# Second layer norm in a feed-forward kernel: its scaling moves to ScalarE, its shift to GpSimd, its tiles to other steps

## The reference, cut to what matters

```python
h = layer_norm(DEEPNORM_ALPHA * h + mix, ln1_g, ln1_b)
ff = (jax.nn.silu(h @ w_ff_gate) * (h @ w_ff_up)) @ w_ff_down
return layer_norm(DEEPNORM_ALPHA * h + ff, ln2_g, ln2_b)

def layer_norm(x, g, b, eps=1e-5):
    mu = jnp.mean(x, -1, keepdims=True); xc = x - mu
    var = jnp.mean(xc * xc, -1, keepdims=True)
    return xc * lax.rsqrt(var + eps) * g + b
```

## Time and profile before

| | us |
|---|---|
| median of 3 runs | 3842.73 (3835.66 to 3848.98) |
| the profiled run: device time | 3841.75 |
| its span, first to last instruction | 3839.5 |
| down stage on PE, from first to last matmul | about 3364 to 3812 |
| after the last matmul | about 3812 to 3839.5 |

### The profile page before, as it was taken

How to read it: one execution, slowest core, us unless ns; L and a number is a source line. 1 busy time by engine, 2 the same in 40 slices (tenths; PEclk the granted TensorE clock), 3 DMA queues, 4 the chain that set the end, 5 groups by cost and what they waited for, 6 DMA issues and landing times. The chain is left out here.

```text
span 3839.5 us, 52628 instructions
## 1 busy us (share of the span) xinstructions
PE 3512.5 (91%) x17866; PEld 2925.5 (76%) x17866; DVE 2162.0 (56%) x2906; ACT 1901.6 (50%) x3569; POOL 1742.2 (45%) x2034
## 2 busy tenths in 40 slices
PE   5998788898979999999997998889999999999896
PEld 4876566676767888989996877678887888888685
DVE  4206666787522365567442665565456545466857
ACT  3213577787624698888554332243334333344342
POOL 5313566665411132222002665556665665454544
PEclk9989899899986999999998999999999999999998
DMA  7324322422221111100004455654445444465562
GB/s 241 150 66 111 83 74 70 157 83 82 88 91 36 40 40 42 35 26 15 19 15 141 144 173 198 212 179 169 153 163 174 164 139 144 156 247 187 207 228 97
DMA packets 327963, 464.23 MB, mean 121 GB/s; under 512 B 22809, under 2 KB 216553, under 8 KB 323849
## 3 DMA queue, kind: packets, MB, share of 16 engines
q1 hardware_dynamic: 301296, 417.88, 32.9%
q10 hardware_dynamic: 26400, 43.00, 3.2%
HBM read 307.02 MB, written 153.78 MB: 120 GB/s over the span
## 5 line engine op out<-in xcount | busy, mean ns | idle before, releaser
L2454 POOL TENSOR_TENSOR ff_rounded_ring<-ff_raw,ff_rounded_ring 128x512 fp32r<-128x512 f32 x264 | 380.2, 1452 | 297.6 <-ACT ff_rounded_ring L2588 295.0
L105 PE MATMUL ff_bank<-ff_rounded_pair,ff_rounded_ring 128*128 128x512 f32 x1232 | 482.8, 392 | 18.6 <-DVE ff_resid L2748 7.6
L106 PE MATMUL ff_bank<-ff_rounded_pair,ff_rounded_ring 128*128 128x512 f32 x1232 | 481.6, 391 | 0.0
L107 PE MATMUL ff_bank<-ff_rounded_pair,ff_rounded_ring 128*128 128x512 f32 x1232 | 481.5, 391 | 0.0
L1643 PE MATMUL at_ctx<-at_p_t,at_c_nat 128*128 128x128 f32 (+1 forms) x2432 | 351.9, 286 | 7.9 <-ACT at_ctx_t L1754 7.0
L1643 PEld LDWEIGHTS at_ctx<-at_p_t,at_c_nat 128*128 128x128 f32 (+1 forms) x2432 | 306.5, 194 | 37.7 <-ACT at_ctx_t L1754 13.0
L1748 ACT ACTIVATE at_p_t<-at_turn 128x512 f32<-128x512 f32 (+4 forms) x416 | 213.1, 544 | 206.5 <-PE at_turn L1621 172.7
L2459 POOL TENSOR_TENSOR ff_rounded_ring<-ff_raw,ff_rounded_ring 128x512 fp32r<-128x512 f32 x154 | 215.3, 1404 | 186.5 <-ACT ff_rounded_ring L2638 186.4
L105 PEld LDWEIGHTS ff_bank<-ff_rounded_pair,ff_rounded_ring 128*128 128x128 f32 x1232 | 232.8, 189 | 69.7 <-POOL ff_rounded_ring L2454 16.3
L2816 DVE TENSOR_TENSOR ff_rounded_a_ring<-ff_f_q,ff_rounded_a_ring 128x512 fp32r<-128x512 f32 x154 | 199.3, 1301 | 135.6 <-ACT ff_rounded_a_ring L2630 134.4
L107 PEld LDWEIGHTS ff_bank<-ff_rounded_pair,ff_rounded_ring 128*128 128x128 f32 x1232 | 232.7, 189 | 49.0
(11 more groups left out here) (360 smaller groups left out, 9095.8 us busy)
## 6 DMA issues: line engine op xcount, KB each, us to landing
f_kept<-ff_resid SPq DMA_DIRECT2D x154, 256.0 KB, 2.5
ff_f_q<-f_kept SPq DMA_DIRECT2D x14, 2816.0 KB, 10.2
pj_raw<-in_w_in SPq DMA_DIRECT2D x50, 512.0 KB, 4.4
proj<-se_row SPq DMA_DIRECT2D x96, 256.0 KB, 2.2
ff_raw<-in_w_ff_gate SPq DMA_DIRECT2D x22, 1024.0 KB, 10.7
ff_raw<-in_w_ff_up SPq DMA_DIRECT2D x22, 1024.0 KB, 6.3
ff_raw<-down_comb SPq DMA_DIRECT2D x88, 256.0 KB, 2.7
ff_raw<-in_w_ff_down SPq DMA_DIRECT2D x66, 256.0 KB, 3.2
```

Source lines behind the costliest of these rows:

```text
L105: pe.matmul(out, lhs_lo, rhs_hi, start=start, stop=False, skip_group_check=goes_on)
L106: pe.matmul(out, lhs_hi, rhs_hi, start=False, stop=False, skip_group_check=goes_on)
L107: return pe.matmul(out, lhs_hi, rhs_lo, start=False, stop=stop, skip_group_check=goes_on)
L2454: pool.tensor_tensor(ring[:, step % RING, 1, :].rearrange("p (k c) -> p k c", c=P), f_operand(it, q, m), f32(ring[:, step % RING, 0, :]).r ...
```

## The change

1. **The norm is split over three engines.** `center` on DVE keeps the statistics and the subtraction with the gain. `scale` on ACT multiplies by the root, `add_shift` on POOL adds the shift; both are 128x1024 in place. The tiles stand at other steps, three and four apart: 67, 70, 74, 78 for `resid[0]` of pass 0, 82, 86, 90, 94 for its `resid[1]`, and 144, 147, 149, 151 for `resid[0]` of pass 1. For a tile at D, DVE centres it in its loop at D, POOL takes the root at D+1, ACT scales at D+2, POOL shifts at D+3, ACT stores at D+5.
2. **The last four tiles.** The statistics of their second half, complete earlier, are taken inside the loop (`half_statistics`, steps 145, 148, 150, 152). After the loop, DVE gathers and centres tile by tile. Tiles 0 and 2 are scaled by ACT and shifted by POOL, tiles 1 and 3 by DVE as before (`scale_and_shift`).
3. **Residuals by tile.** `resid[0]` for pass 1 is asked for in four DMAs of 512 KB, at SP's d = 75, 78, 82, 86, each after the store of that tile. `resid[1]` is still one DMA, at SP's d = 103 instead of 99.
4. **Down operands.** `load_product` goes from SP to ACT (`load_late_product`), still at k = 8 of the issuer's loop. ACT's loop stands three steps later in time than SP's.

```diff
+        after = NI * (NQ - 1)
+        NORMS = {after + k: (0, 0, a) for a, k in enumerate((1, 4, 8, 12))} | {after + k: (0, 1, a) for a, k in enumerate((16, 20, 24, 28))}
+        NORMS |= {after + NI * NQ + k: (1, 0, a) for a, k in enumerate((1, 4, 6, 8))}
+        HALF_STATS = {after + NI * NQ + k: a for a, k in enumerate((2, 5, 7, 9))}
...
+                def load_resid_tile(a):
+                    sp.wait_ge(out_stored[a], 16 + START)
+                    sp.dma_start(resid[0][:, a, :], h1_nat[2][:, a * D:a * D + D]).then_inc(resid_loaded[0], 16)
...
-                    if k == 8 and n + 2 < NPASS * NQ:
-                        load_product(n + 2)
-                    if p == 1 and q == 0 and k == 4:
-                        sp.wait_ge(out_stored[0], 16 * TPG + START)
-                        load_resid(1, 0)
-                    if p == 1 and q == 2 and k == 0:
-                        sp.wait_ge(out_stored[1], 16 * TPG + START)
+                    if NORMS.get(d - 8, (1, 0, 0))[:2] == (0, 0):
+                        load_resid_tile(NORMS[d - 8][2])
+                    if p == 1 and q == 2 and k == 4:
+                        sp.wait_ge(out_stored[TPG], 16 * TPG + START)
                         load_resid(1, 1)
...
+                def add_shift(p, h, a):
+                    pool.wait_ge(scaled2, norm_index(p, h, a) + 1 + START)
+                    pool.tensor_tensor(resid[h][:, a, :], resid[h][:, a, :], ln[1][:, :], ALU.add).then_inc(h2_ready, 1)
...
-                for a in range(TPG):
-                    inverse_root(NG + 2 * NPASS - 1, a)
+                add_shift(NPASS - 1, 0, 3)
+                last = NG + 2 * NPASS - 1
+                inverse_root(last, 0)
+                inverse_root(last, 1)
+                add_shift(NPASS - 1, 1, 0)
+                inverse_root(last, 2)
+                add_shift(NPASS - 1, 1, 2)
+                inverse_root(last, 3)
...
+                def scale(p, h, a):
+                    act.wait_ge(centered2, norm_index(p, h, a) + 1 + START)
+                    act.wait_ge(rstd_ready, TPG * (NG + 2 * p + h) + a + 1 + START)
+                    act.activation(resid[h][:, a, :], resid[h][:, a, :], ACT.Copy, scale=rstd[:, a:a + 1]).then_inc(scaled2, 1)
...
+                    if k == 8 and n + 2 < NPASS * NQ:
+                        load_late_product(n + 2)
+                    if d - 2 in NORMS:
+                        scale(*NORMS[d - 2])
+                    if d - 5 in NORMS:
+                        store_out(*NORMS[d - 5])
...
                 for a in range(TPG):
                     gather(NPASS - 1, NQ - 1, a)
-                dve.drain()
-                for a in range(TPG):
-                    normalize(NG + 2 * NPASS - 1, resid[1], a, h2_ready)
+                    dve.drain()
+                    center(NPASS - 1, 1, a)
+                    if a == 2:
+                        scale_and_shift(1)
+                scale_and_shift(3)
```

83 lines of the change are left out of this document (62 added, 21 removed).

## The result

The changed kernel takes 3822.12 us (median of 8 runs, 3812.79 to 3829.7) against 3842.1 us for the kernel before on the same chip (8 runs). The ratio is 0.9942, 95% interval 0.9931 to 0.9954: 20 us less, where 29.4 were forecast. Its profiled run took 3820.59 us, with a span of 3818.8. Both intervals exclude 1, so the gain is clear of the noise, though it is only 0.6% of the whole. Direction and range were right; the forecast gain was 9 us too large in the first measurement and 6 in the second.

A forecast was written before the change was run, and what follows sets the result against it. PE bounds the down stage, with DVE taking time from it at the norms. Gains of 22.9 + 4.2 + 4.3 less 2 make 29.4 us, giving 3813.3 us against the runs' median; range 3804 to 3830.

The forecast's parts named there:

- The middle and the late loss: Down stage: 22.9 us lost between loops 68 and 145, 4.2 us from loop 145 to the end; both expected gone.
- The tail's chain: After the last matmul: root 3 behind tile 2's shift, then `scale_and_shift(3)`; 23.0 us, gain 4.3, between 2 and 6.
- the residue of 2 us: Stalls left in the down stage from POOL and DVE slowing each other: 2 us, with ends of 0 and 6.
- The losses taken as gone: Down stage: PE's losses around the norms and in the last product, 27.1 us together, less a residue.
- the signs that I had named for being wrong: PE waiting for L2889 in steps 82 to 97, ACT waiting for weights near step 83, or the last stage not shorter.
- those for being right: Among others: no DVE-ended PE idle in steps 67 to 100, clock 1.00 there, no PE pause at pass 0's end.
- The sum per four steps: DVE and POOL work in four loop steps: 10.9 to 11.5 us, up to 0.7 more than available; cover 5.4.
- At step 77 no tile is being centred ... the 6.3 us go as well.: End of pass 0: gathers run as PE's sums come in, so PE's 6.3 us wait for a gather disappears.
- I expect small transfers to be as late next to it as before: DMA: moving the product request to ACT's queue leaves small transfers beside it as late as before; no gain.
- Rival 1: Loop norms: a root holds DVE off as the shift did; gain only 14.4, time 3828; chance 0.12.
- Rival 2: Weights late after SP's longer wait at tile 1: PE pauses some 5 us, gain 22.4, time 3820; chance 0.08.
- Rival 3: Steps 67 to 97: coupling of three engines puts DVE or POOL behind per tile; slower, 3860; chance 0.04.

The follow-up runs named there:

- e3: Changed kernel with the loop's tiles back at the old steps, two apart, the norm still split over three engines; 3820.17 us, ratio 0.9948.
- e4: Changed kernel with the new steps, but DVE alone normalising each whole tile of the loop; 3831.07 us, ratio 0.9972.
- e2: Changed kernel without POOL's shift for the twelve tiles in the loop, whose output lacks that addition; 3809.16 us, ratio 0.9914.
- e9: Changed kernel with four one-element-per-partition powers on POOL in place of each loop tile's shift; 3818.47 us, ratio 0.9938.
- e1: Changed kernel with the product request back on SP, at k = 8 of its own loop; 3821.54 us, ratio 0.9944.
- e10: Changed kernel with each loop tile's shift in two halves on POOL and the pass 0 end gathers ahead of that loop's `low_a`; 3820.62 us, ratio 0.9944.
- e5: Changed kernel with each loop tile's shift in two halves on POOL at successive steps; 3818.48 us, ratio 0.9933.
- e6: Changed kernel with the four gathers at the end of pass 0 put ahead of that loop's `low_a` on DVE; 3818.15 us, ratio 0.9929.
- e11: Changed kernel unaltered, measured again in later rounds; 3818.44 us, ratio 0.9937 to the kernel before.
- e12: Changed kernel with half of each loop tile's shift (columns 512 to 1023) moved from POOL to DVE; 3826.58 us, ratio 0.9953.

## Why the prediction was right, and where its size failed

**Right: what bounded the kernel, and that the split removes it.** The middle and the late loss were waits for DVE at the norms. The late loss is gone whole: 26.18 of 26.2 us busy. e3 and e4 show that it is the split. The tail's chain ended with the predicted pieces in the predicted order, at 23.4 us against 23.0; its gain was 3.9 us against 4.3, within the bounds given. Here some luck was in it: my working had root 1 end 7.5 us after PE; it ended 10.0 us after it, behind the centring of tile 0 (3.27 us, which I had counted as 1.3), and the later pieces made up most of that.

**Failed: the residue of 2 us.** The losses taken as gone were 27.1 us, which from 448.0 leaves 420.9. The down stage took 428.3 and 430.6 us in two profiles: the residue is 7.4 to 9.7 us. My ends for it were 0 and 6, so the total came into the range only because the range was wide. Of the signs that I had named for being wrong, one came: PE still waits for L2889 at step 94 (1.5 us). Of those for being right, two failed: PE pauses at the end of pass 0, and the clock of the stretch is 0.98. Three steps were wrong.

*The sum per four steps compared an average with a cover.* It found DVE and POOL together 0 to 0.7 us short in four steps, and set 5.6 us in eight tiles against a cover of 5.4. But it is the lag within a tile that PE meets at a place without cover. With a shift beside it a `low_a` took 2.88 us, and tile 2 was begun 2.7 us later than in an undisturbed step (T(74) + 5.5 instead of 2.8), partly since ACT stood waiting for a root with the features of the next step behind it, which I had put at nothing. e2 shows the price: without the shift the same stage takes 422.5 us. The Trainium skill, *SBUF — State Buffer*, section "SBUF: two separate sides", gives the rule that a DVE instruction with two SBUF inputs and a GpSimd one that reads SBUF exclude each other for the whole instruction; the row at 3572.42 agrees with it. e9 suggests that this is not the whole price, since PE waited 2.5 us for POOL's low weights there, without any shift in the loop.

*"At step 77 no tile is being centred ... the 6.3 us go as well."* Only 2.3 of them went in the first profile. What I overlooked is that DVE's queue is in order: the gathers stand behind two `low_a` and the centring of loop 74, which even undisturbed end 1.0 us too late (e2 measured 1.2). The nearest tile in step numbers was not the nearest in time.

*"I expect small transfers to be as late next to it as before."* They came later. The weights asked for at 3571.97, behind the product's 2816 KB and a residual tile, landed 13.2 us later (11.0 at most in the kernel before), and ACT waited 4.8 us for them at step 77; at step 89 it waited 6.2 us, and the pause at step 94 stands behind that wait. In all, ACT's waits for weights grew from 35 to 55 us. At the one place that I had worked out, near step 83, ACT did not wait.

**The rivals.** Rival 1, the shared port, gave 3828 for a root that holds DVE off as a shift does. This did not come: a root ran beside a centring that kept its 1.27 us. It is the root that was held off,

```profile
3566.99 1.27 DVE L2829 SCALAR_TENSOR_TENSOR ff_resid<-ff_resid,ff_mv,ff_ln 128x1024 f32<-128x1024 f32 x1
3567.16 1.52 POOL L2446 TENSOR_TENSOR ff_rstd<-ff_ve,ff_half 128x1 f32<-128x1 f32 x1 [0.81 <-DVE ff_ve L2828]
```

for it ended 0.4 us after the centring, and took 1.52 us where it takes 0.55 alone (last section). My sum had taken the 1.52 us as POOL's own work. A milder form of the rival, by the shift alone, is part of the missing gain. The time came to lie between the forecast and this rival. Rival 2, late weights, named 3820 and so the right time, mostly for a wrong reason: the waits for weights did grow, from 35 to 55 us, but the largest pause has none ahead of it. At one place they do take part: ahead of the 1.5 us pause at step 94, ACT had waited 6.15 us for weights, and POOL's shift and two `low_b` came on top. Rival 3 did not come in its size, though its coupling over ACT did, as said. That the move of the product request costs nothing and gains nothing was right in the time (e1: 3821.54 us); the late weights only changed their step.

**The distance.** I gave the steps three and four apart a share in the gain, as free time per tile (4.1 to 5.4 us against 3.0). e3 and e4 show it to be small: 0 to 3 us on top of the split, 4.6 alone.

## What to carry to other kernels

When one engine has no time left at some steps, count not only how much an instruction takes from it, but where its lag meets a consumer without buffer; there the queue of the engine, item by item, gives the delay, and an average over several steps hides it. Work that reads two large tiles from SBUF is not moved off DVE for free by giving it to GpSimd; measure the version without the work (e2) first, since it bounds all rearrangements. And when a pause is removed at one place, look at the whole stage's time before believing the gain, and at who ended each new pause, through to the end of the chain: here three versions took 1.3 to 3.4 us from one pause and gained none, and the releaser that PE's row names for the largest new one (`low_a`) had itself been waiting for a transfer. The same holds for an experiment that should rule a rival out: e1 moved the late weights to the very place that it was to clear of them.

## What the runs showed of the hardware

A power of one element per partition on POOL takes 0.55 us when it starts while DVE runs no instruction with two large SBUF inputs (`low_a`, centring, or scaling with shift). Started behind one, it ended 0.41 us after that instruction. This held for every such start with more than 0.15 us of the DVE instruction left, in the down stages and tails of all fourteen profiles: so the 1.52 us of a root are 1.11 us of waiting for the centring, and the 1.00 us of the first of e9's powers are 0.59 us of waiting for a `low_a`. In e9, the first with DVE idle, the second two with a `low_a` begun 0.14 us behind a power:

```profile
3611.31 0.55 POOL L2447 TENSOR_TENSOR ff_rstd<-ff_ve,ff_half 128x1 f32<-128x1 f32 x1
...
3618.64 3.09 POOL L2478 TENSOR_TENSOR ff_junk<-ff_half 128x1 f32<-128x1 f32 x4
3619.93 0.68 DVE L2896 TENSOR_TENSOR ff_rounded_a_ring<-ff_f_q,ff_rounded_a_ring 128x512 fp32r<-128x512 f32 x1
```

The `low_a` was not held off by the power: it took 0.68 us, as it does alone. So the wait goes one way for so small an operand, and both ways for large ones. The two `low_b` behind e9's powers took 3.85 us (2.99 behind a shift) since the first of them began beside a centring, not because powers stood ahead.

A gather, which reads one tile of SBUF and one accumulator, is not held off by POOL, nor POOL by it. In e9:

```profile
3573.56 3.03 DVE L2924 SCALAR_TENSOR_TENSOR ff_resid<-ff_resid,ff_bank 128x512 f32<-128x512 f32 x4
3573.84 1.28 POOL L2472 TENSOR_TENSOR ff_rounded_ring<-ff_raw,ff_rounded_ring 128x512 fp32r<-128x512 f32 x1
```

The granted clock did not fall behind every pause. At the end of pass 0 the matmuls went on at full distance after pauses of 0.6, 1.2 and 1.8 us (e10, e2, e9). After 2.3 and 2.7 us (e5, e6) the distances of 0.43 us cost 1.7 and 1.3 us more, after 4.0, 3.7 and 4.3 us (changed, e11, e12) 1.7, 2.9 and 2.5. But the length of the pause alone does not decide it: a pause of 2.7 us at step 91 of e10 was followed by matmuls at full distance, and one of 1.9 us at step 8 of e6 by 1.7 us of loss at the lower clock. The pauses of the table therefore do not sum to the stage's loss: 418.9 us (154 x 2.72) and 6.7 of pauses are 425.6, with the 1.7 of the lower clock 427.3, and the stage took 428.3.
